# First block's attention scores: fp32 matmuls replaced by fp32r matmuls on split, stacked queries

## The chip, the cores and the metric

The kernel runs on one core of one Trainium2 chip. The metric is the device time of one execution in microseconds (us); lower is better. A core has five engines with queues of their own: PE (TensorE, matmuls; its weight loads are shown as PEld), DVE (VectorE), ACT (ScalarE), POOL (GpSimd) and SP (SyncE, here only DMAs). They meet through semaphores.

## The reference, cut to what matters

Two transformer-like blocks are computed for 1024 tokens of width 1024, all in float32. The change touches the first mixer's sliding window attention: 8 query heads of 64, 2 key/value heads (so 4 query heads share one key head), blocks of 128 tokens, each with the keys of its own and the previous block.

```python
scores = jnp.einsum('bnqkgd,bnskd->bnkgqs', q, kk).astype(jnp.float32) * (HEAD_DIM ** -0.5)
...
slopes = alibi_slopes(Q_HEADS).reshape(KV_HEADS, GROUP)      # 2 ** -(head + 1)
bias = -slopes[:, :, None, None] * dist.astype(jnp.float32)
scores = jnp.where(valid[None, :, None, None], scores + bias, NEG)
mx = jnp.maximum(jnp.max(scores, axis=-1, keepdims=True), sink)
p = jnp.exp(scores - mx)
p = p / (jnp.sum(p, axis=-1, keepdims=True) + jnp.exp(sink - mx))
out = jnp.einsum('bnkgqs,bnskd->bnqkgd', p.astype(vv.dtype), vv)
```

Queries, keys, values, gates and a pooling branch come from one projection of the normed input.

## The kernel before, in words

**Weights and projections.** Activations lie with channels on partitions and tokens along the free dimension. A weight chunk (128 output channels) comes by two DMAs, a plain one from SP (`load`, L529) and one from POOL that rounds to fp32r (`high`, L680); POOL subtracts for the low part (`low`, L687). Three buffers of each turn round (NW = 3): the load of chunk p waits until chunk p - 3 has been used. PE does three fp32r matmuls per piece, high x high, high x low, low x high (`three`, L800). The input projection has 18 chunks: 0 to 3 queries, 4 keys, 5 values, 6 to 9 the pooling input, 10 to 13 the attention's gates, 14 to 17 the pooling's gates. DVE scales each by the norm and puts it in `P0` (L1916, L1943, L1954). `P0` holds queries of head j of key head 0 on partitions 0 to 63 and of key head 1 on partitions 64 to 127.

**Ahead of the attention.** POOL makes constants one after the other (L646 to L672), each waiting for the one before, and then issues its first weight DMA. DVE computes the pooling windows between the evacuations of chunks 10 to 13 (`windows`, L1921: a copy, one addition per level, two small steps, one combination). `block0` on PE (L913) first turns the values with eight transposes (L917), which DVE copies (L1946); then DVE makes the table of biases, one of 128x256 for each head (L1948). PE also waits for chunk 13's evacuation and for the windows.

**The attention loop** has 16 units: unit t is token block n = t // 2 and key head t % 2, each with four query heads. Its order is written out by hand on each engine. On PE, in unit t: `scores(t + 1)` (four fp32 matmuls over 64 rows, L969), three pairs of matmuls of a pooling gate chunk (`gate_steps`, L800; after the last of them, `pool_mix`, L935), `keys_down(t)` (transposes of the probabilities, L983), another such group, `values(t)` (L995), `turn(t - 1)` (L1005). `scores(t)` waits for `s0_max`, that is for maxima0(t - 1) on DVE, since all units use the same four banks.

On DVE, in unit t: `maxima0(t + 1)` (for each head one instruction that scales the scores, adds the bias and takes the maximum, L1974, then small steps with the sinks, L1979 to L1981), in units 2, 6, 10, 14 the evacuation of a gate chunk (`take_gate`, L1954), `output0(t)` (denominator L1990, reciprocal L1992, four scalings L1997, which wait for `values(t)`), `gate0(t - 1)` (L2007, waits for `turn(t - 1)`).

On ACT, in unit t: the copy of the turned probabilities (L1464, waits for `keys_down(t)`), `weights0(t + 1)` (four exponentials and one for the sinks, L1449 and L1453, wait for maxima0(t + 1)), in units 3, 7, 11, 15 a gate's silu (L1471), with a table load before it and another before the next exponential.

POOL splits a weight chunk whenever PE has finished a gate chunk, in units 2, 6, 10 and 14. After the loop come the mixing of the pooling, the output projection, the second mixer and the second block, whose matmuls take the rest of the time.

## Time and profile before

| what | us |
|---|---|
| median of 3 runs | 2207.45 |
| lowest and highest | 2206.37, 2208.48 |
| profiled execution | 2208.33 |
| its span in the trace | 2206.5 |
| PE busy | 2134.7 |
| DVE busy | 1103.4 |
| ACT busy | 497.4 |
| POOL busy | 760.7 |

The span reaches from the first to the last instruction of the profiled execution; its time has 1.8 us more around it. All durations below are of this execution. Times of day are us from the start of the span. A matmul's record overlaps the next one's, since the ends are modelled and the engine is pipelined: distances between starts tell what one costs. "idle" in brackets is how long the engine stood still ahead of the row and what released it. The granted clock (PEclk) is TensorE's, as a share of 2.4 GHz.

### The profile page before, as it was taken

The page shows a single profiled execution, that of the slowest core. Times are in us where ns is not written, and L with a number is a line of the kernel's source. Part 1 is how long each engine was busy: PE and PEld are TensorE (multiplying, and loading weights), DVE is VectorE, ACT ScalarE, POOL GpSimd, SP SyncE. Part 2 cuts the span into 40 slices and gives each one's busy share as a digit, 9 for nine tenths or more (in the row PEclk, how much of TensorE's full clock was granted, in tenths as well). Part 3 has the DMA queues.
Part 4 walks back from the last instruction along what each step waited for, and adds up shares of the span by engine and source line. Part 5 has one row for each costly group of instructions (what it writes and reads, how often), then busy time and mean ns, then how long its engine had stood idle before and what let it go on. Part 6 is the DMA issues. An engine that isn't in the chain of part 4 may idle for free.

```text
span 2206.5 us, 24032 instructions
## 1 busy us (share of the span) xinstructions
PE 2134.7 (97%) x9720; PEld 1667.1 (76%) x9720; DVE 1103.4 (50%) x1447; ACT 497.4 (23%) x815; POOL 760.7 (34%) x605
## 2 busy tenths in 40 slices
PE   7999999999999998999998999999999999999997
PEld 6887877777876766877886555777888888888886
DVE  6137563779998888141563675352322323313223
ACT  3003553421224413220110544111110100101102
POOL 3221015567766853434243000222222222222220
PEclk9999999999999999999999999999999999999999
DMA  4432017544544523447225441322222222222222
GB/s 177 138 115 72 26 59 245 172 153 145 177 158 151 171 96 115 164 150 239 77 79 143 88 92 39 139 96 77 96 95 96 96 96 96 96 96 96 96 96 105
DMA packets 71085, 259.85 MB, mean 118 GB/s; under 512 B 8960, under 2 KB 9216, under 8 KB 70208
## 3 DMA queue, kind: packets, MB, share of 16 engines
q1 hardware_dynamic: 40064, 148.69, 21.7%
q0 software_dynamic: 29808, 108.54, 13.7%
q8 instruction: 77, 1.26, 0.2%
q10 hardware_dynamic: 1104, 1.10, 0.2%
q14 instruction: 32, 0.26, 0.0%
HBM read 230.80 MB, written 12.65 MB: 110 GB/s over the span
## 4 chain that ended last, share of the span: by engine, by line
PE 65%; issue 22%; DVE 6%; POOL 5%; ACT 1%; DMA 1%; POOLq 0%; DVEq 0%; ACTq 0%
PE PS L800 61%; DVE PS L2087 4%; POOL WL L687 4%; PE PS L1054 2%; DMA WH<-weights 1%; POOL WH L680 1%; DVE OT L2480 0%; PE PS L909 0%; PE PS L901 0%; ACT PS L1609 0%; DVE PS L2120 0%; PE PS L1263 0%; ACT XHM L1402 0%; PE PS L1152 0%; ACT SQH L1524 0%
## 5 line engine op out<-in xcount | busy, mean ns | idle before, releaser
L800 PE MATMUL PS<-XHM,WH 128*128 128x512 f32 (+1 forms) x1976 | 689.2, 390 | 27.5 <-DVE XLM L1863 13.0
L800 PE MATMUL PS<-XLM,WH 128*128 128x512 f32 (+1 forms) x1976 | 672.7, 382 | 0.0
L800 PE MATMUL PS<-XHM,WL 128*128 128x512 f32 (+1 forms) x1976 | 669.7, 380 | 0.0
L680 POOL DMA_DIRECT2D WH<-weights x207 | 119.2, 576 | 1331.2 <-PE PS L800 1315.1
L687 POOL TENSOR_TENSOR WL<-WRAW,WH 128x1024 fp32r<-128x1024 f32 x207 | 502.4, 2427 | 25.0 <-DMA WH<-weights 20.4
L800 PEld LDWEIGHTS PS<-XHM,WH 128*128 128x128 f32 x1976 | 367.8, 190 | 120.7 <-issue 23.3
L800 PEld LDWEIGHTS PS<-XLM,WH 128*128 128x128 f32 x1976 | 374.8, 190 | 79.9 <-issue 3.4
L800 PEld LDWEIGHTS PS<-XHM,WL 128*128 128x128 f32 x1976 | 374.7, 190 | 75.4
L2087 DVE SCALAR_TENSOR_TENSOR PS<-G,TAPW,PS 128x512 f32<-128x512 f32 x348 | 262.7, 755 | 11.7
L2458 DVE TENSOR_TENSOR X<-X,PS 128x1024 f32<-128x1024 f32 x64 | 78.2, 1221 | 243.5 <-PE PS L800 243.5
L2448 DVE SCALAR_TENSOR_TENSOR TM<-PS,RBM 128x1024 f32<-128x1024 f32 x32 | 39.1, 1224 | 246.4 <-PE PS L800 246.4
L800 PE MATMUL PS<-AL,WH 128*128 128x512 f32 x512 | 159.5, 393 | 0.0
L800 PE MATMUL PS<-AH,WH 128*128 128x512 f32 x512 | 158.7, 391 | 0.0
L800 PE MATMUL PS<-AH,WL 128*128 128x512 f32 x512 | 158.2, 390 | 0.0
L1825 ACT ACTIVATE TM<-TM 128x1024 f32<-128x1024 f32 x32 | 33.9, 1061 | 550.3 <-DVE TM L2448 550.3
L800 PEld LDWEIGHTS PS<-AH,WL 128*128 128x128 f32 x512 | 96.1, 188 | 22.0
L800 PEld LDWEIGHTS PS<-AL,WH 128*128 128x128 f32 x512 | 96.2, 188 | 20.9
L800 PEld LDWEIGHTS PS<-AH,WH 128*128 128x128 f32 x512 | 96.2, 188 | 20.3
L1221 PE MATMUL PS<-PT,VX 128*128 128x512 f32 (+4 forms) x224 | 85.3, 482 | 2.9 <-ACT PT L1764 2.9
L2441 DVE TENSOR_TENSOR AL<-TM,AH 128x1024 fp32r<-128x1024 f32 x32 | 84.3, 2654 | 1.1 <-ACT AH L1827 1.1
L742 POOL TENSOR_TENSOR RBM<-RBM,SQH 128x512 f32<-128x512 f32 x58 | 74.9, 1292 | 22.3 <-ACT SQH L1524 21.0
L1872 DVE TENSOR_TENSOR PS<-PS,SQH 128x512 f32<-128x512 f32 x60 | 41.6, 695 | 65.3 <-ACT SQH L1411 64.4
(247 smaller groups left out, 2053.0 us busy)
## 6 DMA issues: line engine op xcount, KB each, us to landing
WRAW<-weights SPq DMA_DIRECT2D x207, 512.0 KB, 3.5
WH<-weights POOLq DMA_DIRECT2D x207, 512.0 KB, 4.5
XTOK<-x SPq DMA_DIRECT2D x8, 512.0 KB, 7.3
x_kept<-X SPq DMA_DIRECT2D x4, 1024.0 KB, 7.7
X<-x_kept SPq DMA_DIRECT2D x8, 512.0 KB, 5.1
x_kept<-X SPq DMA_DIRECT2D x8, 512.0 KB, 7.3
X<-x_kept SPq DMA_DIRECT2D x2, 2048.0 KB, 9.7
out<-OT SPq DMA_DIRECT2D x8, 512.0 KB, 2.6
```

Source lines behind the costliest of these rows:

```text
L680: g.dma_start(WH[:, u, :], weights[WORDER[p]]).then_inc(w_hi[u], 16)
L687: g.tensor_tensor(WL[:, u, :], WRAW[:, u, :], WH[:, u, :].bitcast(F32), ALU.subtract)\
L742: g.tensor_tensor(dst, SSUMH[1], SQH[:, 1, i % 2, :], ALU.add).then_inc(tap_added, 1)
L800: m = nc.tensor.matmul(dst[:, a:b], w, v[:, a:b], start=first and n == 0, stop=last and n == 2)
L1054: m = nc.tensor.matmul(bank(6), diagonal(b, i - TAP_BATCH[part]), G1[:, c, h * HALF + j:(h + 1) * HALF + j], start=i == 0, stop=i == TAPS - 1,
L1221: m = nc.tensor.matmul(o[:, q0 - half * HALF:q0 - half * HALF + w], VX[0:keys, j, c, HD * e:HD * e + P], PT2[n % 3][0:keys, a:a + w], star ...
L1825: nc.scalar.activation(TM[:, j % 2, :], TM[:, j % 2, :], ACT.Square).then_inc(a_sq, 1)
L1872: v.tensor_tensor(so_far if k < KD - 1 else SSUMH[h], so_far, SQH[:, h, k % 2, :], ALU.add).then_inc(h_added[h], 1)
L2087: then(v.scalar_tensor_tensor(out=acc, in0=src, scalar=tap, in1=acc, op0=ALU.mult, op1=ALU.add))
L2441: v.tensor_tensor(AL[:, g % 2, j, :], TM[:, j % 2, :], AH[:, g % 2, j, :].bitcast(F32), ALU.subtract).then_inc(a_split, 1)
L2448: v.scalar_tensor_tensor(out=TM[:, j % 2, :], in0=slot(use + j), scalar=0.0, in1=RB[:], op0=ALU.max, op1=ALU.mult).then_inc(evacuated, 1)
L2458: v.tensor_tensor(X[:, e, :], X[:, e, :], slot(use + e), ALU.add).then_inc(evacuated, 1)
```

## The change

The queries are evacuated with a factor 2 ** (head + 1) (`QSCALE`), so that one distance table `DIST` serves all heads, with 2 ** -(head + 1) as the scale of the maxima step; the table of biases is gone. The scores are computed from fp32r parts: q = qh + ql, k = kh + kl. For each token block and key head, `QS0` holds on the key head's own 64 partitions the high part of four heads' queries and on the other 64 the low part; `KD0` holds the high part of the keys on both halves; `KL0` the low part of the keys. One matmul over 128 rows gives qh kh + ql kh, one over 64 rows adds qh kl. ACT makes the high parts (copies), DVE the low parts (subtractions), and SP moves low queries and high keys to the other half of the partitions by DMAs from SBUF to SBUF. Queries are prepared per token block in two buffers, blocks 0 and 1 ahead of the loop, block m in unit 2m - 3. The transposes of the values move into chunk 11, their copy and the keys' second subtraction between the pooling windows. POOL makes eight more constants.

```diff
--- before.py
+++ after.py
@@ -217,6 +217,7 @@
         o_dist = top[0]
         DIST = fixed("DIST", [P, 2 * P])
         INVC = fixed("INVC", [P, 16])
+        QSCALE = fixed("QSCALE", [P, GROUP])
         o_rt = top[0]
         RT = fixed("RT", [8, P])
         RR = fixed("RR", [8, P])
@@ -232,7 +233,10 @@
         P0 = at("P0", [P, 18, S], area)
         PW = at("PW", [P, 4, P], area + 73728)
         VT0 = at("VT0", [P, NB, P], o_x)
-        BIAS = at("BIAS", [P, HEADS, 2 * P], o_x + 4096)
+        QS0 = [[at(f"QS0_{b}{e}", [P, GROUP, P], o_x + 4096 + 4096 * b + 2048 * e, F32R) for e in range(2)] for b in range(2)]
+        QLOW0 = [at(f"QLOW0_{b}", [P, GROUP, P], o_x + 26624 + 2048 * b, F32R) for b in range(2)]
+        P0R = at("P0R", [P, 18, S], area, F32R)
+        KL0, KD0 = P0R[:, K0, :], (P0R[:, V0, :], P0R[:, GB0 + 3, :])
         YT0 = at("YT0", [P, 2, GROUP * HD], o_x + 12288)
         SS0 = at("SS0", [P, 2, GROUP, 2 * P], o_x + 14336)
         PT0 = at("PT0", [P, 2 * GROUP, P], o_x + 22528)
@@ -336,6 +340,12 @@
         pooled = sem("pooled")
         pool_out = sem("pool_out")
         pool_taken = sem("pool_taken")
+        q0_hi = sem("q0_hi")
+        q0_lo = sem("q0_lo")
+        q0_in = [sem("q0_in0"), sem("q0_in1")]
+        k0_hi = sem("k0_hi")
+        k0_lo = sem("k0_lo")
+        k0_in = sem("k0_in")
         v0_turned = sem("v0_turned")
         v0_ready = sem("v0_ready")
         s0_ready = sem("s0_ready")
@@ -585,7 +595,30 @@
                 sp.dma_start(QM[e][first + 1:first + 2, :].bitcast(F32).rearrange("p (a b) -> p a b", a=NB), MXL[:].bitcast(F32))\
                     .then_inc(mrow_in[e], 16)
 
+            def keys_twice(e):
+
+                own, other = slice(HD * e, HD * (e + 1)), slice(HD * (1 - e), HD * (2 - e))
+                sp.dma_start(KD0[e][other, :].bitcast(F32), KD0[e][own, :].bitcast(F32)).then_inc(k0_in, 16)
+
+            def queries_below(m):
+
+                sp.wait_ge(q0_lo, m + 1)
+                for e in range(2):
+                    own, other = slice(HD * e, HD * (e + 1)), slice(HD * (1 - e), HD * (2 - e))
+                    sp.dma_start(QS0[m % 2][e][other, :, :].bitcast(F32), QLOW0[m % 2][own, :, :].bitcast(F32))\
+                        .then_inc(q0_in[m % 2], 16)
+
             for p in range(P_IN2B + 6):
+                if p == 14:
+                    sp.wait_ge(k0_hi, 1)
+                    keys_twice(1)
+                    queries_below(0)
+                    queries_below(1)
+                    sp.wait_ge(k0_hi, 2)
+                    keys_twice(0)
+                if 17 <= p < 20:
+                    queries_below(2 * p - 32)
+                    queries_below(2 * p - 31)
                 load(p)
                 if 6 <= p < 10:
                     sp.wait_ge(squared, KD)
@@ -671,6 +704,9 @@
                                   pattern=[[-1, 2 * P]], channel_multiplier=1))
             const(g.affine_select(out=DIST[:], in_=DIST[:], compare_op=ALU.is_ge, fill=NEG, base=-1,
                                   pattern=[[1, 2 * P]], channel_multiplier=-1))
+            for e in range(2):
+                for j in range(GROUP):
+                    const(g.memset(QSCALE[HD * e:HD * (e + 1), j:j + 1], 2.0 ** (GROUP * e + j + 1)))
 
             def high(p):
 
@@ -910,12 +946,14 @@
                                          start=True, stop=True, skip_group_check=True)
                 m.then_inc(h_wide[h], 1)
 
-            def block0():
+            def values_turn0():
 
                 pe.wait_ge(evacuated, USE0 + V0 + 1)
                 for b in range(NB):
                     m = nc.tensor.transpose(bank(6, 2)[:, b * P:(b + 1) * P], P0[:, V0, b * P:(b + 1) * P], IDENT[:])
                 m.then_inc(v0_turned, 1)
+
+            def block0():
 
                 pe.wait_ge(evacuated, USE0 + 14)
                 pe.wait_ge(small_in, 16 * 6)
@@ -961,15 +999,20 @@
 
                 def scores(t):
                     n, half = divmod(t, 2)
-                    r = half * HD
+                    own = slice(half * HD, (half + 1) * HD)
                     if t >= 1:
                         pe.wait_ge(s0_max, t)
+                    else:
+                        pe.wait_ge(k0_in, 32)
+                        pe.wait_ge(k0_lo, 2)
+                    if half == 0:
+                        pe.wait_ge(q0_in[n % 2], 32 * (n // 2 + 1))
                     k0 = P if n == 0 else 0
+                    keys = slice((n - 1) * P + k0, (n + 1) * P)
                     for j in range(GROUP):
-                        m = nc.tensor.matmul(slot(0)[:, j * 2 * P + k0:(j + 1) * 2 * P],
-                                             P0[r:r + HD, Q0 + j, n * P:(n + 1) * P],
-                                             P0[r:r + HD, K0, (n - 1) * P + k0:(n + 1) * P],
-                                             start=True, stop=True)
+                        dst = slot(0)[:, j * 2 * P + k0:(j + 1) * 2 * P]
+                        nc.tensor.matmul(dst, QS0[n % 2][half][:, j, :], KD0[half][:, keys], start=True, stop=False)
+                        m = nc.tensor.matmul(dst, QS0[n % 2][half][own, j, :], KL0[own, keys], start=False, stop=True)
                     m.then_inc(s0_ready, 1)
 
                 def keys_down(t):
@@ -1340,7 +1383,8 @@
 
             transposes_in()
             for c in range(14):
-                chunk(c, X_IN0, hooks={3: (lambda: norm_sum(N_PRE0),), 6: (lambda: norm_wide(N_PRE0),)} if c == 2 else None)
+                chunk(c, X_IN0, hooks={2: {3: (lambda: norm_sum(N_PRE0),), 6: (lambda: norm_wide(N_PRE0),)},
+                                       11: {1: (values_turn0,)}}.get(c))
             block0()
             out0()
             in1()
@@ -1435,10 +1479,33 @@
             for k in range(KD):
                 square(N_PRE0, k, X[:, k, :])
             norm(N_PRE0)
+
+            def keys0_hi(e):
+
+                own = slice(HD * e, HD * (e + 1))
+                nc.scalar.activation(KD0[e][own, :], P0[own, K0, :], ACT.Copy).then_inc(k0_hi, 1)
+
+            def queries0_hi(m):
+
+                if m >= 2:
+                    act.wait_ge(s0_ready, 2 * m - 2)
+                for e in range(2):
+                    own = slice(HD * e, HD * (e + 1))
+                    nc.scalar.activation(QS0[m % 2][e][own, :, :], P0[own, Q0:Q0 + GROUP, m * P:(m + 1) * P],
+                                         ACT.Copy).then_inc(q0_hi, 1)
+
+            act.wait_ge(evacuated, USE0 + K0 + 1)
+            keys0_hi(1)
+            act.wait_ge(x0_kept, 16 * 4)
+            queries0_hi(0)
+            queries0_hi(1)
             for c in range(4):
                 act.wait_ge(evacuated, USE0 + 10 + c + 1)
                 g = P0[:, GA0 + c, :]
                 nc.scalar.activation(g, g, ACT.Silu).then_inc(gate_done, 1)
+                if c == 1:
+                    act.wait_ge(v0_turned, 1)
+                    keys0_hi(0)
 
             def weights0(t):
 
@@ -1465,6 +1532,8 @@
                 ins.then_inc(pt0_copied, 1)
                 if t + 1 < UNITS0:
                     weights0(t + 1)
+                if t % 2 == 1 and (t + 3) // 2 < NB:
+                    queries0_hi((t + 3) // 2)
                 if t % 4 == 3:
                     act.wait_ge(evacuated, USE0 + 14 + t // 4 + 1)
                     g = P0[:, GB0 + t // 4, :]
@@ -1911,10 +1980,36 @@
                 add_square(N_PRE0, k)
             norm(N_PRE0)
 
+            dve.wait_ge(consts, 42)
             for c in range(U0 + 4):
                 dve.wait_ge(psum_full, USE0 + c + 1)
-                v.tensor_tensor(P0[:, c, :], slot0(c), RB[:], ALU.mult).then_inc(evacuated, 1)
+                if c < K0:
+                    v.scalar_tensor_tensor(out=P0[:, c, :], in0=slot0(c), scalar=QSCALE[:, c:c + 1], in1=RB[:],
+                                           op0=ALU.mult, op1=ALU.mult).then_inc(evacuated, 1)
+                else:
+                    v.tensor_tensor(P0[:, c, :], slot0(c), RB[:], ALU.mult).then_inc(evacuated, 1)
+
+            def keys0_lo(e):
+
+                own = slice(HD * e, HD * (e + 1))
+                dve.wait_ge(k0_hi, 2 - e)
+                v.tensor_tensor(KL0[own, :], P0[own, K0, :], KD0[e][own, :].bitcast(F32), ALU.subtract).then_inc(k0_lo, 1)
+
+            def queries0_lo(m):
+
+                dve.wait_ge(q0_hi, 2 * m + 2)
+                if m >= 2:
+                    dve.wait_ge(q0_in[m % 2], 32 * (m // 2))
+                for e in range(2):
+                    own = slice(HD * e, HD * (e + 1))
+                    ins = v.tensor_tensor(QLOW0[m % 2][own, :, :], P0[own, Q0:Q0 + GROUP, m * P:(m + 1) * P],
+                                          QS0[m % 2][e][own, :, :].bitcast(F32), ALU.subtract)
+                ins.then_inc(q0_lo, 1)
+
             dve.wait_ge(x0_kept, 16 * 4)
+            keys0_lo(1)
+            queries0_lo(0)
+            queries0_lo(1)
             then(v.memset(PAD[0][:, 0:16], 0.0))
             then(v.memset(PAD[1][:, 0:16], 0.0))
 
@@ -1941,11 +2036,11 @@
                 windows(c)
                 dve.wait_ge(psum_full, USE0 + 10 + c + 1)
                 v.tensor_tensor(P0[:, GA0 + c, :], slot0(10 + c), RB[:], ALU.mult).then_inc(evacuated, 1)
-
-            dve.wait_ge(v0_turned, 1)
-            v.tensor_copy(VT0[:].rearrange("p a b -> p (a b)"), bank(6, 2)).then_inc(v0_ready, 1)
-            for h in range(HEADS):
-                then(v.tensor_scalar(BIAS[:, h, :], DIST[:], 2.0 ** -(h + 1), None, ALU.mult))
+                if c == 1:
+                    dve.wait_ge(v0_turned, 1)
+                    v.tensor_copy(VT0[:].rearrange("p a b -> p (a b)"), bank(6, 2)).then_inc(v0_ready, 1)
+                if c == 2:
+                    keys0_lo(0)
 
             def take_gate(g):
 
@@ -1972,7 +2067,7 @@
                 mx = SMALL[:, 48:52]
                 for j in range(GROUP):
                     ins = v.tensor_tensor_reduce(SS0[:, t % 2, j, k0:], slot(0)[:, j * 2 * P + k0:(j + 1) * 2 * P],
-                                                 BIAS[:, half * GROUP + j, k0:], QK_SCALE, -3e38, ALU.add, ALU.max,
+                                                 DIST[:, k0:], QK_SCALE * 2.0 ** -(half * GROUP + j + 1), -3e38, ALU.add, ALU.max,
                                                  SMALL[:, 48 + j:49 + j])
                 then(ins)
                 sinks_ = SINKS[:, half * GROUP:(half + 1) * GROUP]
@@ -2011,6 +2106,8 @@
             for t in range(UNITS0):
                 if t + 1 < UNITS0:
                     maxima0(t + 1)
+                if t % 2 == 1 and (t + 3) // 2 < NB:
+                    queries0_lo((t + 3) // 2)
                 if t % 4 == 2:
                     take_gate(t // 4)
                 output0(t)
```

## Rows read from the trace of the kernel before

**Rows 1.** The page, busy time and instructions of each engine.

```profile
PE 2134.7 (97%) x9720; PEld 1667.1 (76%) x9720; DVE 1103.4 (50%) x1447; ACT 497.4 (23%) x815; POOL 760.7 (34%) x605
```

**Rows 2.** Windows: stretch, its length, then busy time and instructions by engine, clock, DMA share, GB/s.

```profile
187.00:197.00 10.00, 8.79 (x39) 6.99 (x40) 7.19 (x33) 4.05 (x11) 1.87 (x1) 0.83 0.26 101
197.00:305.00 108.00, 108.00 (x637) 89.58 (x635) 57.00 (x253) 55.42 (x161) 9.20 (x7) 1.00 0.09 30
```

**Rows 3.** Timeline of PE, unit 3 of the attention: start, us, engine, line.

```profile
213.27 1.99 PE L969 MATMUL PS<-P 64*128 64x256 f32 x8
215.19 0.73 PE L800 MATMUL PS<-XHM,WH 128*128 128x512 f32 x2
...
218.97 1.89 PE L995 MATMUL PS<-VT,PT 128*128 128x64 f32 x16
...
221.02 1.99 PE L969 MATMUL PS<-P 64*128 64x256 f32 x8
```

**Rows 4.** Timeline of PE, first weight matmul, and start of the attention.

```profile
21.65 1.19 PE L800 MATMUL PS<-XHM,WH 128*128 128x512 f32 x2 [5.70 <-DVE XLM L1857]
...
188.21 1.22 PE L969 MATMUL PS<-P 64*128 64x128 f32 x8 [1.74 <-DVE VT L1946]
189.36 1.22 PE L800 MATMUL PS<-XHM,WH 128*128 128x512 f32 x2
...
193.78 1.16 PE L969 MATMUL PS<-P 64*128 64x128 f32 x8
```

**Rows 5.** Timeline of PE, a stream of fp32r matmuls of 264 columns.

```profile
851.38 0.28 PE L800 MATMUL PS<-XHM,WH 128*128 128x264 f32 x1
...
856.94 0.28 PE L800 MATMUL PS<-XLM,WH 128*128 128x264 f32 x1
```

**Rows 6.** Timeline of ACT, units 1, 3 and 4, and fp32r copies later.

```profile
205.79 0.21 ACT L1453 ACTIVATE SMALL<-SMALL 128x4 f32<-128x4 f32 x1
...
220.87 1.28 ACT L1471 ACT_TABLE_LOAD   x1
...
225.51 1.02 ACT L1464 COPY PT<-PS 128x1024 f32<-128x1024 f32 x1 [2.29 <-PE PS L983]
...
322.70 4.28 ACT L1402 ACTIVATE XHM<-P 128x512 fp32r<-128x512 f32 x8 [0.24 <-issue]
```

**Rows 7.** Timeline of DVE, units 2 to 4, and fp32r subtractions later.

```profile
212.56 2.11 DVE L1990 TENSOR_TENSOR SMALL<-SMALL 128x4 f32<-128x4 f32 x1
...
220.96 0.86 DVE L1997 TENSOR_SCALAR YT<-PS,SMALL 128x64 f32<-128x64 f32 x4 [2.59 <-PE PS L995]
221.74 0.41 DVE L2007 TENSOR_TENSOR P<-PS,P 128x256 f32<-128x256 f32 x1
223.04 0.42 DVE L1974 CUSTOM_DVE_ANT_0 SS<-PS,BIAS 128x256 f32<-128x256 f32 x1 [0.90 <-PE PS L969]
...
319.32 1.28 DVE L1863 TENSOR_TENSOR XLM<-P,XHM 128x512 fp32r<-128x512 f32 x2
```

**Rows 8.** Timeline of POOL, constants, first subtraction, and one in unit 2.

```profile
6.31 2.45 POOL L666 MEMSET INVC<- 128x1 f32 x16
...
18.07 2.35 POOL L687 TENSOR_TENSOR WL<-WRAW,WH 128x1024 fp32r<-128x1024 f32 x1 [6.24 <-DMA WH<-weights]
...
212.28 2.36 POOL L687 TENSOR_TENSOR WL<-WRAW,WH 128x1024 fp32r<-128x1024 f32 x1
```

**Rows 9.** Timeline of DVE, evacuation of chunks 10 and 13, bias table.

```profile
152.31 1.23 DVE L1943 TENSOR_TENSOR P<-PS,RBM 128x1024 f32<-128x1024 f32 x1 [4.46 <-PE PS L800]
...
185.71 1.22 DVE L1943 TENSOR_TENSOR P<-PS,RBM 128x1024 f32<-128x1024 f32 x1 [0.68 <-PE PS L800]
...
187.98 3.35 DVE L1948 TENSOR_SCALAR BIAS<-DIST 128x256 f32<-128x256 f32 x8
```

**Rows 10.** DMAs of L568 (260 KB, SBUF to SBUF, 64 partitions), issue to landing.

```profile
DMA to landing us min/median/max: 3.0/3.1/8.8
```

## The prediction, made before the changed kernel was run

> **What bounds the kernel now.** I read the page first: PE (TensorE) is busy 97% of the span [rows 1], so a change pays where it shortens PE's own queue, or costs where it makes PE wait. The windows by stage then show the stage that is changed, the attention of the first block: from 197 to 305 us PE is busy for all of its 108 us, at the full clock, while DVE (VectorE) has 57 us of work and ACT (ScalarE) 55 [rows 2]. The DMA engines are nearly idle there. The timeline of PE in one unit (a unit is one token block and one half of the heads, 16 in all) is the main view: scores start at 213.27, the weight matmuls that are laid between start at 215.19, the value matmuls at 218.97, and the next unit's scores at 221.02 [rows 3]. So a unit takes 7.75 us, the scores 1.92 of them, and PE never waits. The timelines of ACT and DVE in the same unit tell how much room they leave [rows 6, 7].
>
> **The scores, the gain.** Four fp32 matmuls of 256 columns leave eight records, 1.92 us or 0.240 us each [rows 3]. The change gives eight fp32r matmuls: four over 128 rows (high and low part of the queries stacked, against the high part of the keys twice) and four over 64 rows (high queries, low keys). The trace has no fp32r matmul over 64 rows and none of 256 columns. The nearest is the stream of 264 columns over 128 rows, each with its own weight load: 46 starts from 851.38 to 856.94, 0.121 us each [rows 5]. Bounds: 8 x 0.117 = 0.94 us (the same, scaled to 256 columns) and 1.92 (nothing gained). I take 0.125 us, a little over the nearest row since row counts alternate, so 1.0 us, and 0.93 saved in each of 14 units: 13.0 us. The two units of block 0 have 128 columns: eight records in 1.16 us with the last one's tail [rows 4], against some 0.9: 0.4 for both. Together **13.4 us**, if nothing else holds PE.
>
> Each of these matmuls is half as long as the ones around it, with a whole weight load. The value matmuls, 64 columns and a load each, start 0.108 us apart (16 in the 1.73 us from 218.97 on [rows 3]), which is about a load alone. Had the stream of 264 columns its loads one by one between the matmuls, a step couldn't be 0.121 us [rows 5]: there they are hidden. The Trainium skill ("TensorE: Matmul & The Clock Gate", Part 3) states that a weight load overlaps a running matmul only where the row groups differ. Here they are the same or overlap, so by that rule the load would come on top and nearly all of the gain would go; the trace disagrees with it for 128 rows, and shows nothing for 64 after 128.
>
> **The constants, a cost at the start.** Eight memsets go into POOL's (GpSimd's) list of constants, ahead of its first weight DMA. Sixteen like them took 2.45 us, so eight take 1.2. POOL's first subtraction waits for that DMA until 18.07 and takes 2.35; PE's first weight matmul starts at 21.65, about a microsecond behind it [rows 4, 8]; between them stands a DVE step that reads SBUF twice and didn't run beside POOL's subtraction. Between 0 (the DMA lands no later, as it shares the engines with the inputs) and 1.8 (DVE now goes first and POOL after it) I take **1.2 us** lost, since everything behind waits in a row.
>
> **Before the attention.** The eight transposes of the values move from the start of the attention into a chunk before; PE does them in either place. DVE copied them behind the last evacuation, made the bias table from 187.98 on, and PE idled 1.74 us before scores(0) [rows 4, 9]. Now DVE has, behind the 13th chunk's evacuation, neither. But one 1.2 us subtraction (low keys) and the copy come earlier on DVE, ahead of the pooling windows of the last group, which PE waits for. The windows ended 0.7 us ahead of the last chunk [rows 9], which itself ends 0.8 later now: scores(0) starts at about 188.3 plus the 1.2 above, a change of 0 (bounds -0.5 and +1.0). The bias table itself was hidden: PE had two gate steps to do while it was built. The evacuations of the query chunks keep their 1.23 us with a scalar more. The six DVE and ACT steps for blocks 0 and 1 lie in front of a chunk's end for which DVE idled 4.5 us [rows 9], and take 4.0 us of DVE; their DMAs, and the weight load on SP's queue behind them, have a chunk of 11 us to land in.
>
> **Inside the loop, the costs.** For each of blocks 2 to 7 ACT gets two copies of 64x512, DVE two subtractions of the same size, and SP two DMAs of 128 KB. By the nearest rows a copy is 4.28/8 = 0.54 us, a subtraction 1.28/2 = 0.64, with overlap 0.69 [rows 6, 7]: 1.1 us on ACT and 1.4 on DVE, in every other unit. The work fits; the order is what counts, since DVE's subtraction waits for ACT's copy, and output0(t), gate0(t-1) and maxima0(t+2) stand behind it on DVE. Walk through unit 3 in the old times: ACT's exponentials end at 220.87, copies to 222.0, subtractions to 223.4; denominators, output and gate need 0.4, 0.86 and 0.41 us more, so maxima0(5) starts at 225.1 and ends at 227.1; before, it started at 223.04 [rows 6, 7]. PE wants its result for scores(6), at 228.76 (221.02 and a unit) less the 0.93 of scores(5), 227.8. It just fits.
>
> ACT in that unit also loads a table and does a gate's silu from 220.87, then idled 2.29 us until 225.51 [rows 6]. Copies (1.1) and PE's saving over that stretch (scores 4 and 5, 1.9) use this up by 0.7, and the copy it delays had 0.15 us more: about 0.5 us at the worst in units 4, 8, 12. I take 0.2 in all.
>
> Unit 1 doesn't fit. There the exponentials end at 206.0 [rows 6], the subtractions at 208.5, and maxima0(3) starts at 210.1. Its four reductions end at 211.5, and its small steps read SBUF twice, as the one at 212.56 that took 2.11 us instead of 0.16 beside POOL's subtraction from 212.28 [rows 7, 8]. POOL's now starts earlier, some 210.4, since PE's chunk does, and lasts to 212.8. So s0_max comes at 213.4, and PE wants scores(4) at 211.2: **2.2 us** of waiting. In units 5 and 9 the same meeting misses by 0.4 us (reductions end at 241.9 in old times, POOL starts at 242.3); a hit costs 1.5 us. I take half a hit, **0.7**.
>
> The DMAs: subtractions of block 3 end at 223.4, scores(6) want them at 227.8, 4.4 us later. Twice the size landed in 3.0 to 3.1 us as a rule, once in 8.8 [rows 10]; the second one leaves 0.6 later: 3.7, hidden by 0.7 us.
>
> **The sum.** 13.4 - 1.2 - 0.2 - 2.2 - 0.7 = 9.1 us. What follows is PE's own queue and shifts as a whole. The profiled execution took 2208.33 us (span 2206.5), 0.9 over the median of 2207.45; against it 2199.2, against the median 2198.3.
>
> **The rivals.**
> A. **DVE and POOL meet in three places**, not one, and the two-engine handshake costs as much again: 3 x 1.5 + 1.5 more than I took, about 2203. For it: misses of 0.4 us. Against: the first one resets the phase.
> B. **Weight loads not hidden**: 0.121 + 0.108 per matmul is 1.83 us per unit, 0.1 saved, 1.3 in all, eaten by the constants: 2207. Against: [rows 5]. This is also the case in which fp32r over 64 rows isn't faster. The rule of the Trainium skill ("TensorE: Matmul & The Clock Gate", Part 3) would come out here.
> C. **The clock**: after the 1.74 us idle PE ran at the lower of its two levels (0.83 granted on average from 187 to 197 [rows 2]), and the two groups of gate matmuls from 189.36 to 193.78 took 4.4 us [rows 4], where two such groups take 3.0 at the upper level: 1.4 us each time. A 2.2 us wait in unit 3 can do the same: 2200 to 2201.
> D. **No loss at all in the loop**: 13.4 - 1.2: 2195.3.
> E. **Slower: the queries' DMA arrives late.** The place is the wait for q0_in ahead of scores(4), (6) to (14), six times. It decides when the later landing is over 4.4 us behind the subtraction, and turns the sign over 6.0. For it: 8.8 us has been seen in a busy stretch [rows 10]. Against: DMA share is 0.09 here [rows 2]. If it lands 6.8 us after its issue, between 3.1 and 8.8, that is 7.4 with the 0.6, and costs 6 x 3.0 = 18: 2216.
>
> **Chances.** Forecast 0.46, A 0.16, B 0.14, C 0.08, D 0.05, E 0.11. The forecast's own range is 2195.5 to 2201.5 (bounds of start and matmul step). A measurement of this kernel tells about 0.2%, 4.4 us, from no change: faster means under 2203.0. Forecast, C, D and half of A are there: 0.66; half of A and B are within: 0.22; E is 0.12 with roundings. The range 2194.5 to 2207.0 leaves out E and little else.
>
> **What would show it.** Eight records of the scores in 1.0 us (right) or 1.8 (B). PE's first weight matmul at 22.9. A PE wait for DVE at scores(4), none or small ones at scores(8) and (12) (A if 1.5 us each). Waits of PE for a DMA at scores: E. Small steps of maxima0 at 2 us. A lower granted clock near unit 3: C. A unit that takes 6.8 us. If PE isn't busy all the time from 215 on, my room for ACT and DVE was wrong.

## The result, and the profile after

The changed kernel takes **2225.64 us** (median of 4 runs, 2224.5 to 2229.74) against 2206.91 for the kernel before in the same session: ratio **1.0085**, 95% interval 1.0073 to 1.0098. It is slower by 18.7 us, where 9 us less were forecast, and it lies above the range of 2194.5 to 2207.0. The profiled execution has a span of 2224.9 us, 18.4 more than the one before.

The page of the changed kernel, busy time of each engine, beside [rows 1]:

```profile
PE 2151.6 (97%) x9720; PEld 1671.2 (75%) x9720; DVE 1113.3 (50%) x1457; ACT 509.1 (23%) x833; POOL 761.5 (34%) x613
```

PE got 16.9 us more to do with as many records, so most of the loss isn't waiting: some matmuls became slower. The windows of the changed kernel beside [rows 2] say the same of the attention: from 197 us on PE is never idle, and the granted clock is lower in both windows (0.68 for 0.83, 0.98 for 1.00):

```profile
187.00:197.00 10.00, 8.12 (x23) 5.91 (x22) 3.88 (x14) 4.08 (x11) 2.94 (x2) 0.68 0.31 105
197.00:305.00 108.00, 108.00 (x587) 85.17 (x586) 61.62 (x255) 57.50 (x157) 8.86 (x6) 0.98 0.16 45
```

I laid the start times of equally numbered matmuls side by side. The first weight matmul is 1.0 us late (22.66 for 21.65), scores(0) 1.4 late (189.58 for 188.21), and the matmuls of out0, the stage behind the attention, start at 331.21 instead of 319.67: 11.5 late. This lateness stays between 10.4 and 12.4 until about 1560 us, and in the last stage (the two-layer feed-forward part, whose moving operands are XHM, XLM, AH and AL) it grows to 18.7. So there are **two losses**: 10 us in the attention, and 7 us in a stage that the change doesn't touch.

**The attention.** Timeline of PE in unit 3 of the changed kernel, beside [rows 3]; L1014 is the stacked matmul over 128 rows, L1015 the one over 64:

```profile
218.33 0.39 PE L1048 MATMUL PS<-IDENT,YT 128*128 128x128 f32 x2
218.48 0.36 PE L1014 MATMUL PS<-P0R,QS 128*128 128x256 f32 x1
218.77 0.38 PE L1015 MATMUL PS<-P0R,QS 64*128 64x256 f32 x1
219.08 0.38 PE L1014 MATMUL PS<-P0R,QS 128*128 128x256 f32 x1
...
220.65 0.38 PE L1015 MATMUL PS<-P0R,QS 64*128 64x256 f32 x1
220.96 0.73 PE L836 MATMUL PS<-XHM,WH 128*128 128x512 f32 x2
```

The steps from start to start are 0.31 us, and eight matmuls take 2.48 us. Four fp32 matmuls took 1.92 [rows 3], so the scores themselves lose 0.56 us. The unit loses less: it takes 8.12 us for 7.74, 0.38 longer. The kernel before had such a change of row count too, between the transposes of L1005 over 128 rows and the scores over 64:

```profile
212.95 0.39 PE L1005 MATMUL PS<-IDENT,YT 128*128 128x128 f32 x2
```

There the first score (213.27 [rows 3]) starts 0.32 us behind the transposes' start, in the changed kernel 0.15 (218.33 to 218.48), where it has 128 rows as well. So fourteen units lose 0.38 us each, 5.3. In the two units of 128 columns eight matmuls take 1.94 us instead of 1.08 (scores(1), at the full clock), and the two units together are 1.6 us longer: 0.74 in the second, and 0.88 in the first, by traces that have it at the full clock (4.93 us with the constants later, 4.05 with the scaled queries alone). The rest is clock. The stretch at the lower clock that follows PE's wait ahead of scores(0) is 6.8 us long instead of 3.4, which adds some 1.5 us there. And in unit 11 (first row 286 us) PE ran at half the clock though it hadn't idled, and the unit took 9.72 us, 1.6 more than its neighbours. The 1.4 us at scores(0), 5.3 + 1.6 for the matmuls and 3.1 for the clock make up the 11.5. The timeline of unit 11, and the window of that stretch (granted clock in the third field from the end):

```profile
285.94 1.02 PE L836 MATMUL PS<-XHM,WH 128*128 128x512 f32 x2
286.76 1.05 PE L836 MATMUL PS<-XLM,WH 128*128 128x512 f32 x2
287.61 1.05 PE L836 MATMUL PS<-XHM,WL 128*128 128x512 f32 x2
288.47 1.60 PE L1026 MATMUL PS<-IDENT,SS 128*128 128x128 f32 x8
```
```profile
286.00:289.50 3.50, 3.50 (x12) 2.81 (x12) 2.37 (x13) 0.00 (x0) 0.00 (x0) 0.53 0.00 0
```

The gate group took 2.53 us (285.94 to 288.47) where one at the full clock takes 1.5.

**The last stage.** PE's groups of instructions, 1600 to 2180 us, kernel before (count, busy us, mean ns of one):

```profile
L800 PE MATMUL PS<-AL,WH 128*128 128x512 f32 x456 | 142.3, 393 | 0.0
L800 PE MATMUL PS<-AH,WH 128*128 128x512 f32 x456 | 141.4, 391 | 0.0
L800 PE MATMUL PS<-AH,WL 128*128 128x512 f32 x456 | 140.9, 390 | 0.0
L800 PE MATMUL PS<-XHM,WH 128*128 128x512 f32 x384 | 120.9, 396 | 0.0
```

The same view of the changed kernel:

```profile
L836 PE MATMUL PS<-AH,WL 128*128 128x512 f32 x448 | 141.3, 397 | 0.0
L836 PE MATMUL PS<-AL,WH 128*128 128x512 f32 x447 | 140.8, 396 | 0.0
L836 PE MATMUL PS<-AH,WH 128*128 128x512 f32 x447 | 139.8, 393 | 0.0
L836 PE MATMUL PS<-XHM,WH 128*128 128x512 f32 x384 | 120.8, 396 | 0.0
```

Same code, same shapes, no idle time, but the matmuls that stream AH or AL are longer by 2 to 7 ns; those of XHM are not. Over the 2599 steps from the 7000th to the 9600th matmul the mean from start to start is 230.24 ns before and 232.72 after, 6.4 us in all. AH and AL lie in the work area behind the fixed tiles, and `QSCALE` is a new fixed tile: its 16 bytes, rounded to 32, move the whole area.

### The profile page after: what moved, and what is told of

It is laid out like the page before. It is cut to its first block, busy times and chain, and to the rows that moved or that the text cites. A ratio compares the mean times of both kernels' runs of the same rounds, so it can differ in the third digit from the quotient of the medians.

```text
span 2224.9 us, 24100 instructions
## 1 busy us (share of the span) xinstructions
PE 2151.6 (97%) x9720; PEld 1671.2 (75%) x9720; DVE 1113.3 (50%) x1457; ACT 509.1 (23%) x833; POOL 761.5 (34%) x613
## 4 chain that ended last, share of the span: by engine, by line
PE 58%; issue 27%; POOL 8%; DVE 5%; ACT 1%; DMA 1%; POOLq 0%; DVEq 0%; ACTq 0%
PE PS L836 54%; POOL WL L723 6%; DVE PS L2184 3%; PE PS L1097 2%; POOL WH L716 1%; DMA WH<-weights 1%; DVE OT L2577 0%; PE PS L829 0%; PE PS L1306 0%; POOL RBM L778 0%; PE PS L945 0%; POOL YG L767 0%; DVE XLM L1926 0%; PE PS L937 0%; DVE X L1975 0%
```

## The experiments

Two theories stood for the attention: the weight loads come on top (rival B, but dearer), or the change of row counts costs by itself. Two for the last stage: the address, or something that the attention leaves behind (clock, order of POOL's weights). Each ratio is to the kernel before, run on the same chip.

### The area moved, nothing else

```diff
 # kernel before
+        FILL = fixed("FILL", [P, 4])
         area = top[0]
```

> The kernel before with a filler of 32 bytes per partition ahead of the big work area, nothing else. Theory 'address': in the changed kernel the matmuls of the MLP stage whose moving tiles AH and AL lie in that area are about 6 ns longer each, which makes some 7 us over the stage, because the new constant moved the area by 32 bytes. Then this kernel is 7 us slower than before (ratio 1.003), its matmul starts in the MLP are 232.7 ns apart on average instead of 230.2, and nothing changes ahead of 1560 us. Rival 'phase': the stage is slower because the loads and POOL's subtractions meet the matmuls at other moments, not because of addresses; then this kernel takes the time of before.

Measured: 2215.39 us (before 2206.91), ratio 1.0034 (1.0024 to 1.0045); mean step of the last stage 232.72 ns, as after. The address theory holds, with no attention changed at all: the step is the same to 0.01 ns.

### A fixed tile of 64 bytes

```diff
 # changed kernel
-        QSCALE = fixed("QSCALE", [P, GROUP])
+        QSCALE = fixed("QSCALE", [P, 4 * GROUP])
```

> The changed kernel with QSCALE padded from 16 to 64 bytes per partition, so that the work area moves by 64 bytes instead of 32. Theory 'address': the MLP stage is back at 230.2 ns per matmul if the cost is one of addresses in steps of 64 bytes, and the kernel is 7 us faster than the changed one, so 11.5 us slower than before (ratio 1.0052). If any shift costs, it stays at 1.0085. Rival 'phase': 1.0085.

Measured: 2225.84 us, 1.0091 (1.0074 to 1.0107); step 232.69 ns. A multiple of 64 bytes doesn't cure it.

### All score matmuls over 128 rows

```diff
 # changed kernel, scores()
-  m = nc.tensor.matmul(dst, QS0[n % 2][half][own, j, :], KL0[own, keys], start=False, stop=True)
+  m = nc.tensor.matmul(dst, QS0[n % 2][half][:, j, :], KL0[:, keys], start=False, stop=True)
```

The sum then has one term more, the low queries times the other key head's low keys.

> The changed kernel, with the second matmul of each head over all 128 rows instead of 64 (it then adds low queries x the other key head's low keys, a term of the size of rounding). Theory 'mixed rows': in the changed kernel a score matmul of 256 columns takes 0.312 us because each one has another row count than the one before it, and so its weight load isn't hidden. Then with equal row counts a step is 0.12 us, the eight take 1.0 us instead of 2.5, a unit 6.7 to 6.9 instead of 8.1, and the kernel comes out 15 to 19 us under the changed one, ratio to before 1.001 or a little less. Rival 'short matmuls': loads can't be hidden behind 256 columns of these tiles at all; then the step stays at 0.3 us and the ratio at 1.0085.

Measured: 2208.44 us, 1.0007 (0.9998 to 1.0017). PE's timeline, unit 4 (unit 3 holds a wait, shown below):

```profile
221.47 0.37 PE L1014 MATMUL PS<-P0R,QS 128*128 128x256 f32 x1
221.68 0.28 PE L1015 MATMUL PS<-P0R,QS 128*128 128x256 f32 x1
221.79 0.28 PE L1014 MATMUL PS<-P0R,QS 128*128 128x256 f32 x1
...
222.40 0.28 PE L1015 MATMUL PS<-P0R,QS 128*128 128x256 f32 x1
222.51 0.63 PE L836 MATMUL PS<-XHM,WH 128*128 128x512 f32 x2
```

Eight take 1.04 us (221.47 to 222.51), 0.12 from start to start behind the first. More rows, the same columns, as many loads and the same order of accumulation, and it is 2.4 times as fast. The records of the weight loads (timeline of PEld) show where the time went. In the changed kernel, unit 3, and then here, unit 4:

```profile
218.77 0.18 PEld L1015 LDWEIGHTS PS<-P0R,QS 64*128 64x128 f32 x1
219.08 0.19 PEld L1014 LDWEIGHTS PS<-P0R,QS 128*128 128x128 f32 x1
```
```profile
221.56 0.19 PEld L1015 LDWEIGHTS PS<-P0R,QS 128*128 128x128 f32 x1
221.68 0.19 PEld L1014 LDWEIGHTS PS<-P0R,QS 128*128 128x128 f32 x1
```

With equal rows the load of the matmul that starts at 221.68 has started at 221.56, 0.12 us ahead. With alternating rows the load starts at 218.77 and 219.08, where its own matmul's record starts too, 0.31 behind the one before. So the load is hidden when the row counts are equal and stands in line when they differ, and its length, 0.18 to 0.19 us, is what a step gained (0.12 + 0.19 = 0.31). The unit comes to 6.58 us, where 6.8 was forecast: 1.16 less than before, since the change of row count ahead of the scores is gone as well. But now the waits of the forecast appear. PE's waits from 188 to 330 us, and the two engines at the first of them (PE, then DVE):

```profile
PE PS L1014 <- DVE SMALL L2076: 5.3, 3, 1.8
```
```profile
213.34 0.56 PE L1014 MATMUL PS<-P0R,QS 128*128 128x256 f32 x1 [1.73 <-DVE SMALL L2076]
213.69 0.42 PE L1015 MATMUL PS<-P0R,QS 128*128 128x256 f32 x1
213.91 0.41 PE L1014 MATMUL PS<-P0R,QS 128*128 128x256 f32 x1
```
```profile
206.58 1.39 DVE L2005 TENSOR_TENSOR QLOW<-P,QS 64x512 fp32r<-64x512 f32 x2 [3.79 <-ACT QS L1494]
208.00 0.16 DVE L2085 TENSOR_TENSOR SMALL<-SMALL 128x4 f32<-128x4 f32 x1
...
211.00 1.88 DVE L2074 TENSOR_TENSOR SMALL<-SMALL,SINKS 128x4 f32<-128x4 f32 x1
...
213.12 0.16 DVE L2076 TENSOR_TENSOR SMALL<-SINKS,SMALL 128x4 f32<-128x4 f32 x1
```

That is the chain of the forecast: DVE waits 3.79 us for ACT's copy, the maxima follow late, and their first small step (0.16 us elsewhere, as that at 208.00) takes 1.88, since POOL's 2.35 us subtraction had begun at 210.50. The Trainium skill ("SBUF — State Buffer", "SBUF: two separate sides") states that a VectorE operation with two SBUF inputs and a GpSimd one that reads SBUF lock each other out for a whole instruction. By that the step would be held until POOL's ends, at 212.85; it ends at 212.88, so the trace agrees, as far as POOL's rough spans tell. Behind each of the three waits the clock also fell: PE's records at 213.69 and after are 0.21 us apart, and from 213.3 to 216.7 the granted clock is 0.51.

### Row counts alternate once, not seven times

```diff
 # changed kernel, scores(): first four matmuls over 128 rows, then four over 64
-  nc.tensor.matmul(dst, QS0[n % 2][half][:, j, :], KD0[half][:, keys], start=True, stop=False)
+  nc.tensor.matmul(dst, QS0[n % 2][half][:, j, :], KD0[half][:, keys], start=j % 2 == 0, stop=False,
+                   skip_group_check=True)
+  for j in range(GROUP):
+      dst = slot(0)[:, j * 2 * P + k0:(j + 1) * 2 * P]
```

> The changed kernel, with the four matmuls over 128 rows of a unit first and the four over 64 rows behind them; same matmuls, two changes of row count per unit instead of eight. Theory 'mixed rows': the step is 0.12 us inside each group and longer only at the two seams, so the eight take some 1.3 us, a unit about 7.0, and the kernel is 12 to 16 us under the changed one (ratio to before 1.001 to 1.003). A rival, 'rows 64': matmuls over 64 rows are slow by themselves; then the four over 64 rows keep 0.3 or more each, the eight take 1.9, and the kernel is 8 us under the changed one. 'Short matmuls': no gain.

Measured: 2218.48 us, 1.0049 (1.0032 to 1.0066), 7 us under the changed kernel. That is less than the 12 to 16 expected, and what the rival 'rows 64' had forecast, so the total can't choose between them. The timeline can. PE, unit 4:

```profile
224.64 0.72 PE L1014 MATMUL PS<-P0R,QS 128*128 128x256 f32 x4
225.29 0.73 PE L1018 MATMUL PS<-P0R,QS 64*128 64x256 f32 x4
225.95 0.73 PE L836 MATMUL PS<-XHM,WH 128*128 128x512 f32 x2
```

Eight take 1.31 us, 0.65 for the four over 128 rows and 0.66 for the four over 64; inside each four the starts are 0.12 us apart, and only at its ends 0.20 to 0.22. So fp32r over 64 rows isn't slow. Three theories fall to one: **each change of row count costs about 0.19 us**, a load's length. The scores' own time shows only a part of it (1.31 against 1.04), since the last change also delays the second gate matmul behind them. Whole units show all of it: 6.97 us against 6.58 is 0.39 for two changes, and 8.12 against 6.58 is 1.54 for the eight of the changed kernel. This run has three waits of PE as well (5.0 us) and 90.3 us at the lower clock over the whole run, against 67.0 before and 70.1 with all rows equal. Row counts explain some 6 of the 10 us above that run (14 x 0.39 and a little for block 0); the 20 us more at the lower clock are the likely rest.

### The constants later

```diff
 # changed kernel, POOL
-            for e in range(2):
-                for j in range(GROUP):
-                    const(g.memset(QSCALE[HD * e:HD * (e + 1), j:j + 1], 2.0 ** (GROUP * e + j + 1)))
...
                 high(p)
+                if p == 1:
+                    for e in range(2):
+                        for j in range(GROUP):
+                            const(g.memset(QSCALE[HD * e:HD * (e + 1), j:j + 1], 2.0 ** (GROUP * e + j + 1)))
```

> The changed kernel with POOL's eight constants for the queries made behind its first two weight DMAs, where POOL stood idle for some 6 us, instead of ahead of them. Theory: they delay everything by their own length, 1.1 to 1.25 us; then PE's first weight matmul is back at 21.7 us from 22.7, the hundredth matmul is 1.25 us earlier than in the changed kernel, and the whole kernel is 1.2 us faster (ratio 1.008). Rival: the inputs' DMAs set that moment and the constants cost nothing; no difference.

Measured: 2224.86 us (before 2206.46), 1.0083 (1.0066 to 1.01). The first weight matmul starts at 21.74 (after: 22.66), as expected. The hundredth was expected 1.25 us earlier and is only 0.25 earlier (32.89 for 33.14), and out0 starts 1.7 earlier (329.51); the stretches at the lower clock lie elsewhere in the two traces, so neither tells the constants' price. In the total the ratio can't be told from the changed kernel's 1.0085.

This trace shows more of the clock: it fell four times in the loop, at 201.4, 242.4, 276.5 and 310.7 us, for 3.4 us each, and PE had no idle time there. The granted clock of one of these stretches:

```profile
242.40:245.80 3.40, 3.40 (x12) 2.72 (x12) 3.23 (x18) 0.00 (x0) 0.00 (x0) 0.50 0.34 77
```

A full unit with such a drop takes 9.7 us instead of 8.12. The next run, with the same order of scores, has three. The kernel before and the other kernels with fp32 scores have none between the start of the loop and its end.

### QSCALE in a gap of the area

```diff
 # changed kernel
-        QSCALE = fixed("QSCALE", [P, GROUP])
+        QSCALE = at("QSCALE", [P, GROUP], area + 75776)
```

> The changed kernel with QSCALE put into 16 unused bytes behind the last tile, so that every tile has the address that it had before. Theory 'address': the MLP's matmul step is back from 232.7 to 230.2 ns and the kernel is 6.5 to 7.5 us faster than the changed one, ratio 1.005; the padding to 64 bytes did not restore it, the old address does. Rival: something else of the change slows the MLP; then the step stays at 232.7.

Measured: 2218.94 us, 1.0056 (1.0039 to 1.0073); step 230.24 ns, exactly as before. Each against its own before, 12.5 us are left of the 18.7: one address was worth 6.2, and the step alone makes 6.4.

### DVE's low parts behind output and gate

```diff
 # the run with 128 rows, DVE's loop over units
-                if t % 2 == 1 and (t + 3) // 2 < NB:
-                    queries0_lo((t + 3) // 2)
                 output0(t)
                 if t >= 1:
                     gate0(t - 1)
+                if t % 2 == 1 and (t + 3) // 2 < NB:
+                    queries0_lo((t + 3) // 2)
```

> The kernel with 128 rows in all score matmuls, and DVE's subtraction for the queries moved behind output0 and gate0 of its unit, instead of ahead of them. Theory 'handshake': in units 1, 5 and 9 DVE stood for ACT's copies, its maxima came late and then met POOL's subtraction, PE waited 1.8 us three times, and the clock fell each time for some 1.5 us more. With the new order DVE uses that time: maxima0(3), (7), (11) are early enough, PE has no wait at scores(4), (8), (12), the drops of the clock at 215, 246 and 277 us are gone, and the loop is 7 to 10 us shorter than with 128 rows alone: ratio to before 0.996 to 0.998. Rival: the wait only moves, since queries now come later and their DMA is late; then PE waits for DMAs instead and the time stays at 1.0007.

Measured: 2200.25 us, 0.9966 (0.9955 to 0.9978). DVE's timeline at the place of the first wait:

```profile
202.71 0.86 DVE L2092 TENSOR_SCALAR YT<-PS,SMALL 128x64 f32<-128x64 f32 x4 [1.78 <-PE PS L1038]
203.48 0.41 DVE L2102 TENSOR_TENSOR P<-PS,P 128x256 f32<-128x256 f32 x1
204.43 1.39 DVE L2005 TENSOR_TENSOR QLOW<-P,QS 64x512 fp32r<-64x512 f32 x2 [0.54 <-ACT QS L1494]
...
207.35 0.16 DVE L2074 TENSOR_TENSOR SMALL<-SMALL,SINKS 128x4 f32<-128x4 f32 x1
...
208.96 1.79 DVE L2085 TENSOR_TENSOR SMALL<-SMALL 128x4 f32<-128x4 f32 x1
```

DVE waits 0.54 us for the copy instead of 3.79, having done its other work first. The maxima are through before POOL begins; POOL now catches the denominators (1.79 us), and PE has no wait in that unit. PE no longer waits for L2076 at all. What it waits for instead is ACT: 0.3 us in units 4, 8 and 12 each, for the copy of the turned probabilities, which stands behind the queries' copies, the table load and the silu; these units take 7.1 us instead of 6.58.

### The scaled queries alone

```diff
 # kernel before, with QSCALE and its memsets; the scores stay fp32; in the four query chunks:
-  v.tensor_tensor(P0[:, c, :], slot0(c), RB[:], ALU.mult)
+  v.scalar_tensor_tensor(out=P0[:, c, :], in0=slot0(c), scalar=QSCALE[:, c:c + 1], in1=RB[:],
+                         op0=ALU.mult, op1=ALU.mult)
-  for h in range(HEADS):
-      then(v.tensor_scalar(BIAS[:, h, :], DIST[:], 2.0 ** -(h + 1), None, ALU.mult))
-  BIAS[:, half * GROUP + j, k0:], QK_SCALE, -3e38
+  DIST[:, k0:], QK_SCALE * 2.0 ** -(half * GROUP + j + 1), -3e38
```

> The kernel before with the scaled queries and the one distance table in place of the table of biases, and nothing else of the change: fp32 scores, no preparation. Theory: the table's 3.1 us on DVE were hidden behind PE's gate steps, so the loop and its start don't move; what is left is the constants' 1.2 us and the 7 us of the moved addresses: 8 us slower than before, ratio 1.0037. Rival: the table held up the first maxima and with them PE; then the loop starts 1 to 2 us earlier and the ratio is 1.003.

Measured: 2215.48 us, 1.0039 (1.0024 to 1.0053), beside 1.0034 for the area moved alone. Giving up the table brings nothing that can be measured in the total. In its profiled execution out0 starts 1.3 us earlier than before, but that one has two stretches less at the lower clock ahead of out0, so I claim no gain from it.

### Which tile, and which remainder

```diff
 # kernel before; first run N = 32, second N = 512
-        AH = at("AH", [P, 2, FG, S], area, F32R)
-        AL = at("AL", [P, 2, FG, S], area + 32768, F32R)
-        TM = at("TM", [P, 2, S], area + 65536)
+        AH = at("AH", [P, 2, FG, S], area + N, F32R)
+        AL = at("AL", [P, 2, FG, S], area + 32768 + N, F32R)
+        TM = at("TM", [P, 2, S], area + 65536 + N)
```

> The kernel of before with only the three tiles of the last stage (AH, AL, TM) 32 bytes further up; every other tile, and all instructions, stay. If it is the address of the moving tiles AH and AL that costs, the mean step of the last stage's matmuls is 232.7 ns instead of 230.2, and the run takes about 2206.9 + 6.5 = 2213.4 us, ratio 1.003. If another tile's address did it in the runs before (the ones that lie in the same area in earlier stages, or the small tiles behind), the step stays at 230.2 ns and the ratio is 1.000.

> The same with 512 bytes instead of 32. If only the remainder of the address by some small power of two (up to 512) matters, the step is 230.2 ns and the ratio 1.000. If any move off this place costs (a distance between tiles that matters, or a larger power of two), it is 232.7 ns and 1.003, as with 32 and 64 bytes.

Measured: 32 bytes 2214.1 us (before 2208.41), 1.0027 (1.0016 to 1.0038), step 232.72 ns; 512 bytes 2207.18, 0.9997 (0.9987 to 1.0006), step 230.24. PE's groups from 1600 to 2180 us, with 32 bytes and with 512 (those of XHM have 396 ns in both):

```profile
L800 PE MATMUL PS<-AH,WL 128*128 128x512 f32 x446 | 140.7, 397 | 0.0
```
```profile
L800 PE MATMUL PS<-AH,WL 128*128 128x512 f32 x457 | 141.3, 390 | 0.0
```

The three tiles of the last stage alone carry the loss. A move by 32 or 64 bytes costs and one by 512 doesn't; if it goes by the remainder of the address by a power of two, that is 128, 256 or 512. The three were moved together, so which of them matters wasn't separated; the longer records are those that stream AH or AL.

### The parts put together

The first of these two has all rows at 128 (with the extra term named above), DVE's new order, the constants later and QSCALE in the gap; the second is the same with the changed kernel's own products, grouped four and four.

> All that the runs showed, put together: 128 rows in all score matmuls, DVE's subtraction behind output0 and gate0, QSCALE in unused bytes so that no tile moves, and its constants behind the first two weight DMAs. By the sum of the parts: 0.9966 for the first two, 7 us less for the addresses (the MLP's matmul step at 230.2 ns), and 0 to 1.2 us less for the constants: 2191 to 2193 us, ratio 0.993. Rival: the parts don't add up, since an earlier PE meets POOL's subtractions at other moments and waits again in the loop; then 2194 to 2198.

> The best version once more, but with the changed kernel's own products: per unit four matmuls over 128 rows and then four over 64 (high queries, low keys), no extra term. If only the number of changes of row count sets the price, each of the 14 full units takes 1.31 us of scores as in the run with grouped matmuls against 1.04 with all 128 rows, and the two of block 0 a little: 14 x 0.27 + 0.4 = 4.2 us over the best version's 2190.9, so 2195.1 us, ratio 0.9947. If the clock drops of that earlier run (90 us at the lower level against 70) belong to the grouped order itself, it is some 2200 us or more, ratio 0.997.

Measured: **2190.89 us** (before 2207.28), **0.9927** (0.9913 to 0.994); and **2195.23 us** (before 2207.53), **0.9949** (0.9936 to 0.9963). Both beat both kernels, and both fall within 0.2 us of what the sum of the parts gave, closer than their spreads let one expect (2189.6 to 2194.68 and 2192.18 to 2200.25). For the second it is luck besides: the sum took 0.27 us a unit for the two changes of row count, the units differ by 0.40 (6.97 for 6.57), and what makes up for it is that the first one's three waits for ACT, of 0.33 us in units of 7.15, don't occur in the second. PE's timeline of unit 3 in the second:

```profile
212.19 0.72 PE L1015 MATMUL PS<-P0R,QS 128*128 128x256 f32 x4
212.83 0.73 PE L1019 MATMUL PS<-P0R,QS 64*128 64x256 f32 x4
...
219.16 0.72 PE L1015 MATMUL PS<-P0R,QS 128*128 128x256 f32 x4
```

A unit is 6.97 us long, 0.77 shorter than before. The grouped order doesn't lower the clock by itself: this profiled execution has 60.0 us at the lower level, none of it between 194 and 305 us. The low clock of the earlier grouped run's loop stood behind its waits, which are gone here.

## Why the prediction was wrong

**The step that failed** is the first term: "I take 0.125 us, a little over the nearest row since row counts alternate, so 1.0 us, and 0.93 saved in each of 14 units: 13.0 us." The row it rested on [rows 5] is right for equal row counts, where I measured 0.12. For alternating ones it is 0.31, the load on top. 13.4 us saved was forecast for all scores and 6.9 lost came (14 x 0.38 and 1.6): 20.3 of the 27.8 us between the forecast change (9.1 less) and the measured one (18.7 more). The address adds 6.4. The 3.1 us of waits that were forecast for the loop and didn't come are made up by 3.1 of clock that the sum didn't have. About 1 us is left. The upper bound was wrong as well. "1.92 (nothing gained)" is no bound at all, since nothing in the trace excluded a loss. And the kind of step in question was in the trace of before, at each end of the scores: the 0.32 us from 212.95 to 213.27, shown above.

**Rival B** named the right mechanism, loads that aren't hidden, and the page that speaks for it, and put its price at 0.229 per matmul; it was 0.312, so B came out level with the kernel before (2207) and not slower. The price failed at the load: 0.108 us was read off the distance of the value matmuls as "about a load alone". But their loads overlap one another too, and the page of the kernel before has a load's own length, 190 ns:

```profile
L800 PEld LDWEIGHTS PS<-XHM,WH 128*128 128x128 f32 x1976 | 367.8, 190 | 120.7 <-issue 23.3
```

With it B would have been 0.121 + 0.190 = 0.311 per matmul and 2.49 us per unit, where 2.48 was measured. The rule of the Trainium skill ("TensorE: Matmul & The Clock Gate", Part 3), that a load overlaps a running matmul only where the row groups differ, gets a mixed verdict. For 128 rows behind 128 and for 64 behind 64 the trace disagrees with it (starts 0.12 us apart); the same part also lets a load into the background weight buffer go ahead, which would allow this. For 64 behind 128 and 128 behind 64 the loads aren't hidden, as the rule says of groups that overlap. I held its agreement in the one case for disproved by the other.

**The address** was missed altogether, and cost 6.4 us. That the new tile `QSCALE` moves all behind it was readable in the diff, but no row of the trace of before could have priced it.

**The constants:** 1.2 us forecast, 1.0 at the first weight matmul: right there. In the total no run can tell them from nothing. "PE's first weight matmul at 22.9" came at 22.66. **Before the attention:** scores(0) at 189.5 forecast, 189.58 measured; that close is luck, since six other traces with the constants in the same place have it anywhere from 188.44 to 190.01. **The table** hidden: right, as far as the total can tell.

**DVE, POOL and the wait:** right in mechanism and place, and invisible in the changed kernel, since slow scores gave DVE 0.4 us more per unit than before (8.12 for 7.75) rather than 0.93 less. Once they were fast, PE waited 1.73 us at the first place (2.2 forecast), and also at both of the others, where I had "half a hit". That is **rival A**, and the lower clock of **rival C** came with it. The run with equal rows, less 6.4 for the address, is 2202, against 2203 in rival A. That closeness is in part luck: the gain was 1.16 us a unit where 0.93 was forecast, and the clock, which A doesn't count, fell three times. **The copies on ACT** do cost PE time in units 4, 8 and 12, as forecast: "about 0.5 us at the worst", and 0.5 to 0.6 it was each time in the runs with the new order on DVE, where the sum took 0.2 in all.

**Rival E** had the right sign for the wrong reason. PE never waited for a DMA at the scores; the queries' DMAs landed in 2.3 us at the median of the changed kernel's DMA view.

**What stays open:** why an address off by 32 or 64 bytes makes these matmuls longer, and by which power of two (128 and 256 weren't tried); whether it is the number of rows that must be equal or the rows themselves, since no run was made that puts a matmul over rows 0 to 63 behind one over rows 64 to 127; and why the clock falls while PE is busy with alternating matmuls. That goes with the alternating order, but the traces don't say by what.

## What to carry to other kernels

Keep the number of rows the same from one matmul to the next, or group the matmuls by it: here, together with DVE's new order, it turned a stage's loss of 10 us into a gain, even at the price of computing rows that aren't needed. Take the price of an unhidden load from the load's own record, not from the distance of matmuls whose loads may overlap. Put a small new tile where it moves nothing, and when a stage that wasn't touched gets slower with the same code and no idle time, compare the addresses of its operands. And when the nearest row differs from the new operation in one respect, that respect is the risk: the bound on its side goes past "nothing gained".

## What the runs showed of the hardware

- An fp32r matmul of 256 columns starts 0.12 us behind the one before where both have 128 rows or both 64, and 0.31 us where 128 and 64 alternate. Each change of row count costs 0.19 us, the length of a load's record, and that record starts ahead of its matmul's in the one case and together with it in the other. Four fp32 matmuls of the same shape take 1.92 us, so alternating high and low parts (2.48) is slower than not splitting at all.
- Streaming an operand of 512 columns whose tile is 32 or 64 bytes off takes 2.5 ns more per matmul on average over the stage (230.24 to 232.72), 6.4 us over 2599 of them; at 0 or 512 bytes the mean is the same to 0.01 ns.
- PE's waits in the loop of 1.58 to 1.78 us (three with equal rows, three in the first grouped run) were each followed within 2 us by a stretch at the lower clock of 3.4 us or, once, 6.8. The idle of 1.7 to 1.9 us ahead of scores(0) was so followed, within some 3 us, in ten of fourteen traces and not in the other four (the constants later, the new order on DVE, the scaled queries alone, the tiles moved by 512 bytes).
- With alternating row counts the clock also fell while PE was busy: once, once, four and three times in the loops of the four kernels that have them, and never in the loops of the five with fp32 scores, nor in those of the three that have equal or grouped rows and the new order on DVE.
